# The last 24 score units of a hybrid decoder block contract in two halves of 64 rows, each half with a PSUM bank of its own

## The reference, cut to what matters

```python
def peer_ffn(xn, w_query, sub_keys, expert_u, expert_v):
    ...
    e1 = jnp.take_along_axis(i1, ci // PEER_TOPK, axis=-1)
    e2 = jnp.take_along_axis(i2, ci % PEER_TOPK, axis=-1)
    idx = e1 * N_KEYS + e2
    gate = jax.nn.softmax(best, axis=-1)
    ...
        act = jax.nn.gelu(jnp.einsum('cd,ced->ce', xc, expert_u[ic]), approximate=False)
        return jnp.einsum('ce,ced->cd', (gc * act).astype(xc.dtype), expert_v[ic])
```

## Time and profile before

| | |
|---|---|
| median of 3 runs | 5064.34 us (5059.01 to 5066.17) |
| profiled execution | 5060.61 us |
| its span | 5058.9 us |
| TensorE busy | 4931.4 us (97%) |
| DVE busy | 2690.3 us (53%) |
| ACT busy | 1377.5 us (27%) |
| POOL busy | 1875.1 us (37%) |
| granted TensorE clock, mean | 0.989 |

### The profile page before, as it was taken

How to read it: one execution, slowest core, us unless ns; L and a number is a source line. 1 busy time by engine, 2 the same in 40 slices (tenths; PEclk the granted TensorE clock), 3 DMA queues, 4 the chain that set the end, 5 groups by cost and what they waited for, 6 DMA issues and landing times.

```text
span 5058.9 us, 71629 instructions
## 1 busy us (share of the span) xinstructions
PE 4931.4 (97%) x27458; PEld 3962.0 (78%) x27458; DVE 2690.3 (53%) x3970; ACT 1377.5 (27%) x1294; POOL 1875.1 (37%) x479
## 2 busy tenths in 40 slices
PE   7999999998999999999999999999999999999998
PEld 5777777776878777888877777788888888888887
DVE  3343334343545335778466666620266666666667
ACT  3222222222222122222233333322222222222222
POOL 4222222222334433444433333334344444444443
PEclk9999999998999999999999999999999999999999
DMA  3222222221234322222333434334334443434442
GB/s 120 80 80 80 76 80 82 78 80 57 88 115 142 141 83 105 106 107 106 114 137 137 155 139 151 143 140 148 129 127 147 142 148 141 140 128 147 143 156 91
DMA packets 182653, 595.95 MB, mean 118 GB/s; under 512 B 11616, under 2 KB 77408, under 8 KB 129136
## 3 DMA queue, kind: packets, MB, share of 16 engines
q1 hardware_dynamic: 150688, 506.09, 28.2%
q10 hardware_dynamic: 31824, 87.72, 4.4%
HBM read 508.28 MB, written 85.48 MB: 117 GB/s over the span
## 4 chain that ended last, share of the span: by engine, by line
PE 77%; issue 10%; DVE 7%; ACT 2%; POOL 2%; DMA 1%; ACTq 1%; DVEq 0%; POOLq 0%; SPq 0%
PE ps L311 14%; PE ps L313 13%; PE ps L312 13%; PE ps L1717 9%; PE ps L1718 9%; PE ps L1719 9%; PE ps L1413 3%; DVE oh L1233 2%; POOL wl L306 2%; DVE stage L1241 1%; ACT stage L867 1%; DVE oh L1229 1%; DVE ysb L1039 1%; ACT wh L302 1%; PE ps L1678 0%
## 5 line engine op out<-in xcount | busy, mean ns | idle before, releaser
L306 POOL TENSOR_TENSOR wl<-raw,wh 128x2048 fp32r<-128x2048 f32 x396 | 1838.6, 4643 | 3113.8 <-ACT wh L302 3113.8
L311 PE MATMUL ps<-xh,wh 128*128 128x512 f32 x3904 | 1579.6, 405 | 39.3 <-DVE xl L946 18.9
L313 PE MATMUL ps<-xh,wl 128*128 128x512 f32 x3904 | 1546.5, 396 | 0.0
L312 PE MATMUL ps<-xl,wh 128*128 128x512 f32 x3904 | 1545.9, 396 | 0.0
L302 ACT ACTIVATE wh<-raw 128x2048 fp32r<-128x2048 f32 x396 | 758.4, 1915 | 1884.7 <-PE ps L313 1407.6
L311 PEld LDWEIGHTS ps<-xh,wh 128*128 128x128 f32 x3904 | 739.4, 189 | 226.1 <-issue 39.7
L313 PEld LDWEIGHTS ps<-xh,wl 128*128 128x128 f32 x3904 | 738.4, 189 | 174.1
L312 PEld LDWEIGHTS ps<-xl,wh 128*128 128x128 f32 x3904 | 739.6, 189 | 169.6 <-issue 8.3
L1717 PE MATMUL ps<-wh,gah 128*128 128x512 f32 x2048 | 809.3, 395 | 0.0
L1718 PE MATMUL ps<-wh,gal 128*128 128x512 f32 x2048 | 808.0, 395 | 0.0
L1719 PE MATMUL ps<-wl,gah 128*128 128x512 f32 x2048 | 808.0, 395 | 0.0
(11 more groups left out here) (299 smaller groups left out, 3569.4 us busy)
## 6 DMA issues: line engine op xcount, KB each, us to landing
raw<-stream SPq DMA_DIRECT2D x396, 1024.0 KB, 4.8
gelu_scratch<-preb ACTq DMA_DIRECT2D x128, 256.0 KB, 2.0
gates_scratch<-stage ACTq DMA_DIRECT2D x16, 2048.0 KB, 6.6
gt<-gates_scratch SPq DMA_DIRECT2D x32, 1024.0 KB, 6.0
act<-gelu_scratch SPq DMA_DIRECT2D x32, 1024.0 KB, 8.6
mergegate_scratch<-sgb ACTq DMA_DIRECT2D x32, 256.0 KB, 2.0
sgm<-mergegate_scratch SPq DMA_DIRECT2D x32, 256.0 KB, 2.7
h_in<-x_t SPq DMA_DIRECT2D x4, 1024.0 KB, 9.0
```

Of the source, the lines that this page charges most:

```text
L306: pool.tensor_tensor(wl[s][:, :], raw[s][:, :], wh[s][:, :].bitcast(F32), ALU.subtract).then_inc(w_lo, 1)
L311: pe.matmul(dst, w_h, h[:, kx, :], start=start, stop=False)
L312: pe.matmul(dst, w_h, l[:, kx, :], start=False, stop=False)
L313: return pe.matmul(dst, w_l, h[:, kx, :], start=False, stop=stop)
```

## The change

The last 24 score units no longer use `ahead`. Each of the 48 matmuls of a unit becomes two, of the upper and the lower 64 contraction rows, on the same 128 columns and 512 tokens. The upper halves accumulate in bank 4 or 5, the lower ones in bank 6 or 7, upper and lower alternating. ACT now copies the lower half's bank to preb, DVE adds the upper half's bank to it, and ACT applies Gelu from preb to preb before the store. The 22 adds of the loop stand on DVE ahead of the gated parts of group 0, and the last two adds between these and the low parts of group 0.

```diff
             def rest(e, s):
-                act_ahead(e, s, score_unit(SC_REST) + e - SC_REST)
+                n = score_unit(SC_REST) + e - SC_REST
+                act.wait_ge(w_used, n + 1)
+                split_hi(act, n + 2, s)
+                act.wait_ge(pre_stored[s], 8 * e + 16 - 8 * s)
+                act.activation(preb[:, s, :], bank(6 + s), ACT.Copy).then_inc(lower_copied, 1)
+                act.wait_ge(halves_added, e - SC_REST + 1)
+                own(act, act.activation(preb[:, s, :], preb[:, s, :], ACT.Gelu), pre_ready, e + 1)
+                act.dma_start(act_d[bass.ds(e, 1)].rearrange("a p t -> p (a t)"), preb[:, s, :]).then_inc(pre_stored[s], 16)
...
+            def add_halves(e, s):
+                dve.wait_ge(lower_copied, e + 1)
+                dve.tensor_tensor(preb[:, s, :], bank(4 + s), preb[:, s, :], ALU.add).then_inc(halves_added, 1)
+
+            with dve.Fori(0, (NKEYS - SC_REST) // 2 - 1) as i:
+                for s in range(2):
+                    add_halves(2 * i + s, s)
             for e in range(GE):
                 dve_gated(0, 0, e)
+            for s in range(2):
+                add_halves(NKEYS - SC_REST - 2 + s, s)
             for e in range(GE):
                 dve_low(0, 0, e)
...
+            def ahead_halves(e, s, n):
+
+                pe.wait_ge(pre_ready, e - 1)
+                pe.wait_ge(w_lo, n + 1)
+                for k in range(KT):
+                    for m, (w, x) in enumerate(((wh, xh), (wh, xl), (wl, xh))):
+                        for r in range(2):
+                            half = slice(CH * r, CH * r + CH)
+                            last = pe.matmul(bank(4 + 2 * r + s), w[s][half, k * P:(k + 1) * P], x[half, k, :],
+                                             start=k == 0 and m == 0, stop=k == KT - 1 and m == 2)
+                last.then_inc(w_used, 1)
+
             with pe.Fori(0, (NKEYS - SC_REST) // 2) as i:
                 for s in range(2):
-                    ahead(SC_REST + 2 * i + s, s, score_unit(SC_REST) + 2 * i + s)
+                    ahead_halves(SC_REST + 2 * i + s, s, score_unit(SC_REST) + 2 * i + s)
```

More of the change, by code:

```diff
@@ L282, in build @@
         best_ready, ex_ready, routed, egt_ready, egt_saved = sem("best_ready"), sem("ex_ready"), sem("routed"), sem("egt_ready"), sem("egt_saved")
+        lower_copied, halves_added = sem("lower_copied"), sem("halves_added")
         gate_split, oh_ready, oh_used, dense_upper, dense_saved = (sem(n) for n in ("gate_split", "oh_ready", "oh_used", "dense_upper", "dense_saved"))
```

## The result

The changed kernel takes 5076.74 us in the median of 11 runs (5068.63 to 5079.84), the kernel before 5064.34 (5059.01 to 5066.17). The ratio is 1.0024, 95% interval 1.0015 to 1.0034, which is 8 to 17 us slower. Forecast was 5076 us, slower, in a range from 5055 to 5100.

What follows compares the result with a forecast made beforehand. TensorE was taken as the bound, busy 97% of the span, with no later idle stretch to absorb delay. Handover 9.5 + clock 2.0 + pairs 0 gave +11.5 us on 5064.3, so 5076 us, range 5055 to 5100.

Steps and rivals of the forecast that it cites:

- Pairs at 0: In the 24 score units, each pair of half matmuls takes as long as one whole matmul: 0 us, no gain.
- (a): Rival: in the 24 units the halves run one after the other in fp32r, 267.6 us plus 11.5, 5343 us; chance 0.12.
- (b): Rival: in the 24 units matmuls overlap but weight loads do not, 165.5 us plus 11.5, 5241 us; chance 0.04.
- the forecast's own range: Whole time if pairs overlap with a handover wait of 6 to 10 us: 5056 to 5096 us, chance 0.77.
- The entry: Where TensorE enters 64-row work: a single cost of about 0.1 us, dropped from the sum.
- Steps in each unit: After each score unit, ACT's copy, DVE's add and Gelu take 3.7 us, hidden because TensorE needs the banks 11.15 us later.
- Step 1: After unit 22 of 24, the delayed gating of group 0 (L1265) still leaves 1.4 us of cover: no cost.
- Step 2: After unit 24, low parts wait behind the last add and POOL's hold, so TensorE idles 9.5 us.
- Step 3: TensorE's restart after the handover idle runs at a reduced clock, costing 2.0 us.
- Nothing given back: Downstream of the handover, in the values, nothing recovers the lost time.

Runs made afterwards that it cites:

- experiment 1: Changed kernel with DVE's last two adds moved behind the four low parts of group 0; 5061.96 us against 5061.96 for the kernel before, ratio 1.0002.
- experiment 7: Changed kernel without the lower halves' matmuls, ACT copying the upper half's bank instead (result not the reference's); 5077.96 us in one run.
- experiment 3: Changed kernel in which ACT, in the last score unit, copies and applies Gelu before splitting the next weights; 5068.81 us, ratio 1.0014 to the kernel before.
- experiment 2: Kernel before, whole matmuls, with DVE waiting for the last Gelu before the low parts of group 0; 5081.15 us against 5061.96, ratio 1.0032.
- experiment 5: Changed kernel with all 48 upper-half matmuls of a unit ahead of the 48 lower-half ones; 5309.74 us, ratio 1.0488 to the kernel before.
- experiment 6: Changed kernel with the halves alternating in groups of twelve matmuls; 5187.05 us, ratio 1.0245 to the kernel before.
- experiment 4: Changed kernel with the halves alternating in threes; 5075.09 us against 5061.96 for the kernel before, ratio 1.0029.
- experiment 8: Kernel before with the low parts of group 0 made late by a DVE wait, run again to look at the values; 5079.75 us in one run.

## Why the prediction was right

- **Pairs at 0.** Right. It was read from f32 matmuls of quarters, and fp32r halves of all 128 columns behave alike: pitch 0.232 us as for whole ones, no gain and no loss beyond 0.3 us (experiment 1). Rivals (a) and (b) are excluded by the trace: matmuls and loads run in pairs, 0.19 to 0.20 us for two loads (185 ns each, a load of 128 rows 188). No run shows the 19.9 us by which the forecast's own range reaches to either side, 17 ns for each of 1152 pairs; the runs have 0.232 us for whole matmuls, for pairs and for one half alone (experiment 7). The entry, dropped at 0.1, is 0.2 us.
- **Steps in each unit.** Right, and hidden: Gelu ends 3.8 us after the unit (split at 3603.89, Gelu until 3607.67), 3.7 forecast. POOL does not hold the add: 691 ns in the mean of 23.
- **Step 1, cover of 1.4 us.** Right: ACT has the high parts done at 3591.29, the next split comes at 3592.74 after 1.45 us of idle.
- **Step 2, 9.5 us.** 9.2 measured (3612.78 against 3603.36 and a pitch of 0.23). The step was right in mechanism, POOL's hold included (experiment 3); I had put 0.25 us between the last low part and TensorE's start, most of it a load, and the trace has 0.06 (3612.72 to 3612.78).
- **Step 3, the clock, 2.0 us.** The two stretches of the earlier trace rows hold 46 and 45 matmuls in 12.5 us, where 12.5 / 0.2323 is 54, so they lose 1.8 and 2.0 us. The term was too small: from the residual matmul's start to the start of the kernel's last matmul it takes 1444.5 us, before 1441.7, 2.8 more. Before, the two restarts ran at a granted clock of 0.50 for 4.0 and 4.2 us, here it is 5.7; the 12.5 us have granted clock 0.76, not 0.84. The length of the idle time does not give this price: experiment 2 restarts after the same 9.0 us and is at a granted clock of 1.00 after 3.2 us (0.87 in its 12.5 us), and experiment 3 idles only 3.8 us and needs 4.9 (0.80). Two rows were too few for a term to a tenth of a us.
- **Nothing given back.** Right: the values run at 11.15 us a unit on both sides.

The errors, -0.3, +0.8 and +0.2, add up to 0.7: 11.5 forecast, 12.2 in the trace, 12.2 by the ratio. The mechanism was right in each step. That the median agrees to 1 us is partly luck, given a spread of 11 us between runs; and a trace whose values run at 11.20 us, as in four of the experiments, is some 6 us longer, which the forecast had no term for.

## What to carry to other kernels

When work is added to an engine that also prepares the next stage, place it by the whole program's deadline: two adds of 0.7 us stood ahead of four instructions whose inputs had been ready for 15 us (3591.29 to 3606.92), and cost 12 us of TensorE. When such an instruction becomes late, look at what it now shares its moment with; here it fell into another engine's 4.5 us instruction, and the stretch from the restart on, at first at a granted clock of 0.50, took 2.8 us more. Splitting a contraction in two row halves was free here only where the halves alternated closely (11.15 us a unit singly or in threes, 15.82 in twelves), and it brought nothing: a pair had the pitch of one whole matmul, 0.232 us.

## What the runs showed of the hardware

- Matmuls of the two row halves did not all start in program order: they passed each other by three to four (3.5 pitches at each change of half, from 20.65 and 15.82 us a unit in experiments 5 and 6; at 11.15 us a unit in experiment 4 every pair overlapped).
- In the changed kernel a DVE instruction with two SBUF inputs, begun while POOL's split (two SBUF inputs as well) ran from 3605.88 to 3610.38 us, took 4.00 us in place of 0.68 and ended at 3610.92, while the add with a PSUM and an SBUF input beside the same POOL instruction took its 0.69. The values of the changed kernel show it in most units, without cost: the gated part (L1273) has a median of 3.91 us there, as from 4001.50 to 4005.41 us beside POOL's split from 4000.24 to 4004.86.
- 48 whole fp32r matmuls took 11.20 us in the values of experiments 2, 4, 5 and 8 and 11.15 in those of the other six traces, as the median and nearly throughout; what chooses is open.
- After an idle time of 9.0 us the granted clock was 0.50 for 3.2 us (experiment 2) to 5.7 us (changed kernel).
